# Normalizing the next subgroup at the end of the current projection stream, in a four-layer hybrid trunk on eight cores

## The reference, cut to what matters

```
h = rmsnorm(x, g1);  u, v, bgate, cgate, hb, z, xbc, dt = split(h @ w_in)
x = x + concat([chunk_mlp(u, v), bgate*conv(cgate*hb), rmsnorm(ssd(silu(conv(xbc)), dt)*silu(z))]) @ w_out
x = x + square(relu(rmsnorm(x, g2) @ w_ff1)) @ w_ff2
```

## Time and profile before

| | |
|---|---|
| median of 2 runs | 5696.12 us (5580.25 to 5811.99) |
| the profiled execution, its own time | 5409.83 us |
| its span on the slowest core (core 1) | 5408.1 us |
| spans of the eight cores | 5341.3 to 5408.1 us |
| mean granted TensorE clock of the cores | 0.865 to 0.873 |
| busy share of the span, TensorE matmul | 76% |
| VectorE / ScalarE / GpSimd | 37% / 28% / 13% |

### The profile page before, as it was taken

One profiled execution on the slowest core, in us unless ns is written; L12 is line 12 of the kernel. 1 busy time (PEld: TensorE's weight loads), 2 busy tenths in 40 slices (PEclk: granted clock), 3 DMA queues, 4 the chain that ended last, 5 costly groups with the idle time before them and its releaser, 6 DMA issues.

```text
span 5408.1 us, 83387 instructions; the slowest of 8 cores (5341.3 to 5408.1 us)
## 1 busy us (share of the span) xinstructions
PE 4106.9 (76%) x29164; PEld 2854.0 (53%) x29164; DVE 1980.3 (37%) x4852; ACT 1516.3 (28%) x3631; POOL 714.4 (13%) x956
## 2 busy tenths in 40 slices
PE   4679767966886785788787787866698698798785
PEld 3455555545554553556565555545455455555553
DVE  2343334323333433333433433333433343433432
ACT  2231323133222321422323314214313223322321
POOL 1011001200210111021111120110111111121110
PEclk9789968977896897889899898878799799898887
DMA  8155615740582348077365583690555555356344
GB/s 118 43 65 61 101 30 65 91 89 17 73 105 72 42 58 131 5 88 96 48 79 63 65 96 37 82 122 20 66 63 63 63 66 63 46 70 76 45 51 54
DMA packets 763803, 363.70 MB, mean 67 GB/s; under 512 B 439018, under 2 KB 709484, under 8 KB 763396
## 3 DMA queue, kind: packets, MB, share of 16 engines
q0 software_dynamic: 646016, 295.82, 46.1%
q1 hardware_dynamic: 117380, 62.54, 4.7%
HBM read 625.29 MB, written 28.76 MB: 121 GB/s over the span
## 4 chain that ended last, share of the span: by engine, by line
PE 63%; DVE 12%; ACT 8%; DMA 8%; issue 7%; POOL 1%; DVEq 0%; ACTq 0%; SPq 0%; POOLq 0%
PE bk L1049 16%; PE bk L1029 15%; PE bk L592 7%; PE bk L997 4%; DMA ring<-w_ff 3%; DVE scr L523 3%; PE bk L693 2%; PE bk L783 2%; PE bk L784 2%; ACT scr L508 2%; PE bk L513 2%; PE bk L734 2%; PE bk L772 2%; PE bk L898 1%; PE bk L851 1%
## 5 line engine op out<-in xcount | busy, mean ns | idle before, releaser
L1029 PE MATMUL bk<-scr,ring 128*128 128x384 bf16 (+1 forms) x6144 | 996.7, 324 | 32.7 <-DMA ring<-w_ff 23.8
L1049 PE MATMUL bk<-scr,ring 128*128 128x384 bf16 (+1 forms) x6144 | 960.2, 317 | 0.7 <-issue 0.4
L1029 PEld LDWEIGHTS bk<-scr,ring 128*128 128x128 bf16 x6144 | 611.5, 100 | 406.6 <-issue 69.7
L1049 PEld LDWEIGHTS bk<-scr,ring 128*128 128x128 bf16 x6144 | 601.1, 98 | 346.4 <-issue 3.6
L1033 ACT ACTIVATE scr<-bk 128x384 bf16<-128x384 f32 (+1 forms) x768 | 362.6, 473 | 1463.6 <-PE bk L1029 1437.0
L482 POOL DMA_DIRECT2D ring<-w_ff x384 | 354.0, 922 | 3048.5 <-PE bk L592 1616.4
L592 PE MATMUL bk<-scr,ring 128*128 128x256 bf16 (+1 forms) x5120 | 606.1, 275 | 29.6 <-DMA ring<-w_in 14.4
L1055 DVE TENSOR_TENSOR xT<-xT,bk 128x384 f32<-128x384 f32 (+1 forms) x768 | 408.4, 532 | 506.5 <-PE bk L1049 506.5
L1035 DVE TENSOR_TENSOR scr<-scr 128x384 bf16<-128x384 bf16 (+1 forms) x768 | 265.5, 347 | 724.2 <-ACT scr L1033 714.4
L592 PEld LDWEIGHTS bk<-scr,ring 128*128 128x128 bf16 x5120 | 476.1, 105 | 93.4 <-issue 35.9
L485 POOL DMA_DIRECT2D ring<-w_ff x384 | 229.1, 597 | 817.3 <-PE bk L1049 817.3
(11 more groups left out here) (129 smaller groups left out, 4118.4 us busy)
## 6 DMA issues: line engine op xcount, KB each, us to landing
ring<-w_ff POOLq DMA_DIRECT2D x768, 256.0 KB, 14.6
ring<-w_in POOLq DMA_DIRECT2D x132, 512.0 KB, 16.9
ring<-w_out POOLq DMA_DIRECT2D x48, 512.0 KB, 24.6
scr<-ssm SPq DMA_DIRECT2D x64, 256.0 KB, 2.9
oss<-scr SPq DMA_DIRECT2D x64, 256.0 KB, 2.3
yp<-scr SPq DMA_DIRECT2D x7, 1024.0 KB, 11.7
xT<-xp SPq DMA_DIRECT2D x2, 2560.0 KB, 12.0
rowsT<-rows SPq DMA_DIRECT2D x12, 268.0 KB, 5.0
```

The lines of the kernel that those rows point to most:

```text
L1029: i_ = e.matmul(hp[:, 0:n], lhsT=sub(ring[:], s_ * 2048 + k * 128, [[1, 128]]), rhs=h2[:, k, c0:c0 + n], start=(k == 0), stop=(k == 7))
L1049: i_ = e.matmul(op_[:, 0:n], lhsT=sub(ring[:], sl[hc] * 2048 + 1024 + oc * 128, [[1, 128]]), rhs=hid[:, hb_, hc, 0:n], start=(hc == 0), st ...
```

## The change

There are three edits. First, `hT` becomes two buffers, `hT2`, taken in turn by subgroups; to make room the intermediate `lnv` of the norm shares its memory with `rstd`. Second, the norm is split off from `stream_A` as `stream_Apro`. It runs by itself for the first subgroup, and the `stream_A` of subgroup i issues the `stream_Apro` of subgroup i+1 as its last steps. Third, in `prep_compute` the transposes of v = 1 use bank `bk6`, so that v = 0 and v = 1 no longer share a bank.

```diff
-        hT = carve([8, N], BF16)
-        lnv = carve([N])
+        hT2 = [carve([8, N], BF16) for _ in range(2)]
         rstd = carve([N])
+        lnv = rstd
...
+                bkt_ = bk7 if v == 0 else bk6
+                bkn_ = "bk7" if v == 0 else "bk6"
...
-                P.op("pe", tr, reads=rd, writes=["bk7"])
+                P.op("pe", tr, reads=rd, writes=[bkn_])
...
-        def stream_A(gi, l, sg):
+        def stream_Apro(gi, l, sg):
             tiles, slots, c0, n, is_s, par = sg["tiles"], sg["slots"], sg["c0"], sg["n"], sg["sample"], sg["par"]
+            hT = hT2[par]
             xtok = [("xT", t, k) for t in slots for k in range(8)]
             for _ in rmsnorm_steps(xT[:, :, c0:c0 + n], lambda k: xT[:, k, c0:c0 + n], "g1", l,
-                                   sq, ssq_ps, "bk2", lnv, rstd, lambda k: hT[:, k, 0:n], n, xtok, ["hT"], "nA"):
+                                   sq, ssq_ps, "bk2", lnv, rstd, lambda k: hT[:, k, 0:n], n, xtok, [("hT", par)], "nA"):
                 yield
             yield
+
+        def stream_A(gi, l, sg, pro_next=None):
+            tiles, slots, c0, n, is_s, par = sg["tiles"], sg["slots"], sg["c0"], sg["n"], sg["sample"], sg["par"]
+            hT = hT2[par]
             wl = lambda i: wslot((gi, l, "win", i))
...
+            if pro_next is not None:
+                for _ in stream_Apro(gi, l, pro_next):
+                    yield
...
-                run_streams([Strm(stream_A(gi, l, sgs[0]))])
+                def mkA(i_):
+                    return Strm(stream_A(gi, l, sgs[i_], sgs[i_ + 1] if i_ + 1 < len(sgs) else None))
+                run_streams([Strm(stream_Apro(gi, l, sgs[0]))])
+                run_streams([mkA(0)])
...
-                    nxt = Strm(stream_A(gi, l, sgs[si + 1])) if si + 1 < len(sgs) else None
+                    nxt = mkA(si + 1) if si + 1 < len(sgs) else None
```

More of the change, by code:

```diff
@@ L562, in prep_compute, with tr @@
                 rd = ["ws_nat", "cmat"] if v == 0 else ["ws_nat1z", "cmat"] + [("ws_blk", b) for b in range(16)]
-                def tr(e, src_t=src_t):
+                bkt_ = bk7 if v == 0 else bk6
+                bkn_ = "bk7" if v == 0 else "bk6"
+                def tr(e, src_t=src_t, bkt_=bkt_):
                     for h in range(4):
-                        i = e.matmul(bk7[:, h * 128:(h + 1) * 128], lhsT=src_t[:, h, :], rhs=ident, start=True, stop=True)
+                        i = e.matmul(bkt_[:, h * 128:(h + 1) * 128], lhsT=src_t[:, h, :], rhs=ident, start=True, stop=True)
                     return i
-                P.op("pe", tr, reads=rd, writes=["bk7"])
-                P.op("dve", lambda e, v=v: e.tensor_tensor(
-                    wmT[:, v, :, :], bk7[:].rearrange("p (h t) -> p h t", h=4),
+                P.op("pe", tr, reads=rd, writes=[bkn_])
+                P.op("dve", lambda e, v=v, bkt_=bkt_: e.tensor_tensor(
+                    wmT[:, v, :, :], bkt_[:].rearrange("p (h t) -> p h t", h=4),
                     sub(cm_U[v], 0, [[0, 4], [1, 128]]), ALU.mult),
-                    reads=["bk7", "cmat"], writes=[("wmT", v)])
+                    reads=[bkn_, "cmat"], writes=[("wmT", v)])
         def layer_prep(l):
@@ L594, in mm @@
                     return i
-                return mm, rtok(s_) + ["hT"]
+                return mm, rtok(s_) + [("hT", par)]
             pi = [0]
@@ L606, in mmd @@
                     return i
-                P.op("pe", mmd, reads=["hT", "wdt"], writes=["bk2"])
+                P.op("pe", mmd, reads=[("hT", par), "wdt"], writes=["bk2"])
                 P.op("dve", lambda e: e.tensor_tensor(dtr, pdt_ps, rowsT[:, 0:8], ALU.add),
@@ L629, in mmv @@
                     return i
-                P.op("pe", mmv, reads=["hT"] + rtok(sv), writes=["bk2"])
+                P.op("pe", mmv, reads=[("hT", par)] + rtok(sv), writes=["bk2"])
                 P.op("act", lambda e, ti=ti: e.activation(vb[par][:, ti, :], pv_ps, AF.Gelu),
@@ L695, in mmz @@
                     return i
-                P.op("pe", mmz, reads=["hT"] + rtok(sz[0]) + rtok(sz[1]), writes=["bk2"])
+                P.op("pe", mmz, reads=[("hT", par)] + rtok(sz[0]) + rtok(sz[1]), writes=["bk2"])
                 P.op("act", lambda e, ti=ti: e.activation(zs[par][:, ti, :], pz_ps[:], AF.Silu),
```

## The result

The change made the kernel slower: a median of 5627.64 us over 11 runs, against 5478.82 us over 10 runs of the kernel before. The ratio is 1.0338, with a 95% interval of 1.0282 to 1.0393; 5721 us and 1.0044 had been forecast. The profiled execution spans 5586.5 us (core 4) against 5408.1 us.

A forecast was written before the change was run, and what follows sets the result against it. FFN phases were taken as bound by TensorE's work, mixer phases by waits between engines. Moved norms +93 us and bank -69 gave +24 on 5409.8 us, ratio 1.0044, so 5721 us; range 5615 to 5840.

The forecast's parts named there:

- second rival: Slower case: each new mixer-phase stall brings a longer half-clock stretch, 4 us instead of 0.6; ratio 1.023, chance 0.17.
- second subgroup's norm, groups 1 and 2, first rounds: End of the first `stream_A`: norm now precedes `stream_B`, displacing decay work; 7.5 us per layer, eight layers, +60 us.
- third subgroup's norm, groups 1 and 2: End of the first round: decay matmuls start later, less what the second round returns; +14 us (-25 to +35).
- group 0, all norms: Group 0's moved norms, four layers: second subgroup +20 us, third -30 (-7.5 per layer), fourth +17.
- lower clock level: Float32 matmuls behind some 20 new stalls run partly at half clock; 0.6 us each, +12 us.
- bank: FFN phases, second transposes on `bk6`: the 6.97 us wait for VectorE goes, 11 times; -69 us (-45 to -80).
- The chain as such: Norm at the end of `stream_A`, Square to first projection with a table load: 9.1 us for 256 columns, 6.5 for 128.
- The 2 us that I took off for cover from `stream_B`: End of first round, groups 1 and 2: `stream_A` ends earlier relative to `stream_B`, so 2 us (0 to 5) less delay.
- I take 8.2 - 0.7 = 7.5 us per layer: First rounds, groups 1 and 2: displaced TensorE decay work less the earlier projection; eight layers, +60 us.
- In return the wait of 4.98 us at the next first projection goes: Second round, groups 1 and 2: a freed wait with norm matmuls and slow-clock work returns 8 us (group 2), 4.5 (group 1).
- The rival of the clock: New mixer-phase stalls pull TensorE's clock down, 4 us per stall instead of 0.6; ratio 1.023 or 5829 us, chance 0.17.
- The rival that the norms find cover: Later rounds, groups 1 and 2: moved norms lie within `stream_B`; ratio 0.987 or 5622 us, chance 0.18.

The follow-up runs named there:

- no_norm: Kernel before with the bank edit, norms of all subgroups but each layer's first left out; ratio 0.9928 to the kernel before.
- bank_again: Kernel before with the bank edit alone, run once more in five rounds; ratio 0.9848 to the kernel before.
- own_stream: Changed kernel, but second subgroup's norm back in its old place and later norms made streams of their own; ratio 0.9907 to the kernel before.
- own_stream_late: `own_stream` with the modelled time of `stream_A` put forward by the norm's modelled time from the second round on; ratio 0.987 to the kernel before.
- second_only: Changed kernel with only the second subgroup's norm moved, later norms at the head of their own `stream_A`; ratio 1.0197 to the kernel before.
- second_back: Changed kernel with the second subgroup's norm back at the head of its `stream_A`, later norms still moved; ratio 1.0122 to the kernel before.
- filler: Changed kernel with 24 more matmuls, read by nobody, behind each of the 40 norms' own matmuls; ratio 1.0328 to the kernel before.
- decay_then_proj: Changed kernel with `stream_B`'s first-round decay steps issued behind the norm and ahead of `stream_A`; ratio 1.0366 to the kernel before.

## Why the prediction was wrong in size

The direction within the mixer and FFN phases was right, and so was each chain. The sizes of three terms were not, and the forecast of "within 2%" fell with them. That 5627.64 us lies between my bounds of 5615 and 5840 us is luck: these were worked out on a base of 5696.12 us, the median of two runs, and that of the kernel before over ten runs is 5478.82 us. As ratios my bounds are 0.986 and 1.025. The measured 1.0338 lies outside them, and above my second rival's 1.023 as well. The measured values are differences between the two profiled executions.

| step of the sum | forecast | measured |
|---|---|---|
| second subgroup's norm, groups 1 and 2, first rounds | +60 | +111 |
| third subgroup's norm, groups 1 and 2 | +14 | +65 |
| group 0, all norms | +7 | +75 |
| lower clock level | +12 | in the above |
| bank | -69 | -70 |
| sum | +24 | +181 |

*The chain as such* was right: 9.1 us forecast from Square to projection, 8.95 measured, and the table load comes behind the wait. The stalls are where they were expected: 5.9 us at the projection of the first round, and at its end the next decay matmuls start 8.7 us later than before in group 1 (11.03 us after the start of the last convolution instead of 2.30) and 11.3 us later in group 2 (13.59 instead of 2.30), both as worked out. The 2 us that I took off for cover from `stream_B` did not show in these starts. The Trainium skill (ScalarE: Activation LUTs, What ACT_TABLE_LOAD costs) has 1380 ns of drain on top of each load of 1283 ns. Here the load starts 0.09 us after the matmuls end and the Ln at 3016.90, 1.29 us after the load began, so the measurement decides: no such drain in this chain.

*First place, +60 against +111.* The step that failed is "I take 8.2 - 0.7 = 7.5 us per layer": it counted the displaced work and took the rest of the round to be unchanged, with the order of the two streams as before. `no_norm` shows the rest. With no moved norm at all, but in the changed kernel's order, the first round of group 1 is 4.3 us longer than in `bank_again` and that of group 2 6.9 us (58.5 against 51.6). The exposed chain adds the other 8 to 10 us. So about 5 us of the 14 us per round are the new order of the two streams, which was not in my sum; the convolution's new wait of 4.3 us is there in both kernels. Taking the two parts as a sum is an estimate.

*Later places, +14 against +65.* The new stall was sized well; the return was not. The step that failed is "In return the wait of 4.98 us at the next first projection goes": I booked -4.5 us per layer in group 1 and -8 in group 2 for it. The wait did go, but others came. `own_stream` and `own_stream_late` too remove much of that wait and gain nothing. With a return of 0 my own numbers give 6.7 us per layer in group 1 and 9.3 in group 2, +64 us in all. That this is so near +65 is chance, as by groups it does not fit: the second and last rounds together grew by 9.7 us in group 1 and by 6.1 in group 2. In group 1 part of it is the order again: `no_norm`, without these norms, is 3.9 us longer there than `bank_again`, with the wait for L649; in group 2 it is not longer.

*Group 0, +7 against +75.* The two versions that move only part of the norms split it. With the second subgroup's alone (`second_only`) the first two rounds together are 8.5 us longer per layer (layers 2 to 4), my upper bound of 8 and not my 5. The sample tile's first YD matmul (L842 before, L853 after) comes 40.1 us into the layer before and 58.2 us after. That fits the reading by which its chain sets the end, but 18 us later at the start are 9 us at the end, so the chain alone does not show it. With only the later norms moved (`second_back`) these rounds are 1.2 us shorter, where -7.5 was booked for the third subgroup's: that return, the largest single term in my sum for group 0, never came. In the fourth subgroup's place the round is 10 us longer, where 4.2 was the net forecast.

*The rival of the clock* looked as if it had won, since the total is on its side and the lower level took 1361 us of the mixer phases instead of 1062. `filler` speaks against it: 134 us less of it changed nothing, and TensorE's longer busy time is at most 55 us of the loss. The stalls did add time at the lower level, but the time of the kernel did not hang on most of it. *The rival that the norms find cover* fell: at the end of the first round `stream_B` and `stream_A` end within 1 us of each other (L880 at 3075.91 and L742 at 3076.75 in group 1), and behind them there is nothing to cover with.

*The bank* came out as worked out: 2.2 us of waiting forecast and 2.58 measured after four blocks. That the sum agrees to 1 us is luck, as other pairs of profiled executions give 60 to 99 us.

What stays open is how much of the 5 us by the new order belongs to which queue. With 16 table loads less (`decay_then_proj`) the time did not fall, but I did not test the order with the norm's chain held fixed, nor the kernel without the norms in the order of before, which alone would show what a hidden norm is worth there.

## What to carry to other kernels

A chain that hops between engines, one link at a time, should stand where other work lies between its links in every queue. At the end of a stream it was bare here, however early that is; and in one block ahead of the other work or behind it, it was bare too. Before a wait is removed, ask what the removal brings with a version that leaves the work out altogether: here even that gained nothing, in the order that was then built, and neither did any place that I tried. And where a model settles the order of instructions when the program is built, each edit of a stream changes the order of all of them, and the trace has to be read for that before the edit is blamed.

## What the runs showed of the hardware

A stretch at the lower clock was not worth its length: 134 us less of it (1361 to 1227 us on core 4), brought about by matmuls with no reader, left the mixer phases at 3253 us, and the program's own matmuls were only 12 us shorter in all. A table load took 1283 ns every time, and a version with 16 fewer of them in the mixer phases, though in another order, was no faster.
